# Output product on pairs of weight chunks, and other places for the second norm's steps, in a streaming encoder layer

## The reference

```python
def _mixers(h, st, p):
    ...
    merged = (g[:, :, 0] * (y_a @ p['w_br_ssd']) + g[:, :, 1] * (y_b @ p['w_br_gla'])
              + g[:, :, 2] * (y_c @ p['w_br_ml']))
    return merged @ p['w_out'], (...)

def _layer(x, c, st, p):
    ...
    x = x + g1 * _rmsnorm(mix, p['g_post_mix'])
    h = _rmsnorm(x, p['g_pre_ffn']) * (1.0 + sc2) + sh2
    f = (jax.nn.silu(h @ p['w_ffn_gate']) * (h @ p['w_ffn_up'])) @ p['w_ffn_down']
    x = x + g2 * _rmsnorm(f, p['g_post_ffn'])
```

## Time and profile before

| | |
|---|---|
| median of 3 runs | 1731.3 us (1730.98 to 1731.34) |
| the profiled execution's own time | 1731.23 us |
| its span, first to last instruction | 1729.0 us |
| PE busy | 1682.0 us, 97% |
| DVE busy | 1013.5 us, 59% |
| ACT busy | 641.3 us, 37% |
| output product, first matmul to the FFN's first | 1221.56 to 1285.36 us of the span |

### The profile page before, as it was taken

The page is one execution under the profiler, slowest core; times in us unless marked ns, Lnnn a source line. Parts: engine busy times, 40 slices in busy tenths (PEclk is TensorE's granted clock), DMA queues, the critical chain, the costliest instruction groups (busy, mean ns, idle before and its releaser), DMA issues.

```text
span 1729.0 us, 29185 instructions
## 1 busy us (share of the span) xinstructions
PE 1682.0 (97%) x11296; PEld 1543.6 (89%) x11296; DVE 1013.5 (59%) x1860; ACT 641.3 (37%) x1306; POOL 86.4 (5%) x160
## 2 busy tenths in 40 slices
PE   6999999999999999999999999999999999999997
PEld 4879898787899997899998899999999999999996
DVE  3745356644655554443533434555667788878886
ACT  5423333333433332333434343232343343343342
POOL 0000000000222220000000000000010000000001
PEclk8999999999999999999999999999999999999998
DMA  9862233575344346844546846445341223233224
GB/s 343 310 218 88 98 114 108 163 214 189 135 155 132 106 133 205 266 143 149 164 162 199 267 165 215 156 152 171 87 133 50 74 76 96 76 96 91 81 74 158
DMA packets 237752, 259.79 MB, mean 150 GB/s; under 512 B 14791, under 2 KB 212871, under 8 KB 235568
## 3 DMA queue, kind: packets, MB, share of 16 engines
q1 hardware_dynamic: 213550, 228.88, 41.6%
q10 hardware_dynamic: 24066, 29.06, 4.8%
HBM read 196.73 MB, written 61.17 MB: 149 GB/s over the span
## 4 chain that ended last, share of the span: by engine, by line
PE 57%; issue 29%; DVE 3%; PEld 3%; DMA 2%; ACT 1%; DVEq 1%; SPq 1%; POOLq 0%; POOL 0%; ACTq 0%; PEldq 0%
PE pj_acc L478 10%; PE pj_acc L480 10%; PE pj_acc L479 10%; PE pj_acc L490 5%; PE pj_acc L492 5%; PE pj_acc L491 5%; PE mx L1944 2%; PEld pj_acc L480 1%; PEld pj_acc L478 1%; PEld pj_acc L479 1%; PE mx L2432 1%; DMA hd_w<-in_w_ada 1%; PE mx L2423 1%; PE mx L2478 1%; PE mx L2703 1%
## 5 line engine op out<-in xcount | busy, mean ns | idle before, releaser
L478 PE MATMUL pj_acc<-pj_act_hi,pj_lo 128*128 128x320 f32 x1176 | 378.6, 322 | 2.1 <-DVE pj_lo L397 1.0
L480 PE MATMUL pj_acc<-pj_act_hi,pj_hi 128*128 128x320 f32 x1176 | 363.4, 309 | 0.0
L479 PE MATMUL pj_acc<-pj_act_lo,pj_hi 128*128 128x320 f32 x1176 | 363.1, 309 | 0.0
L478 PEld LDWEIGHTS pj_acc<-pj_act_hi,pj_lo 128*128 128x128 f32 x1176 | 220.9, 188 | 23.3 <-issue 19.9
L479 PEld LDWEIGHTS pj_acc<-pj_act_lo,pj_hi 128*128 128x128 f32 x1176 | 221.0, 188 | 3.8 <-issue 3.3
L480 PEld LDWEIGHTS pj_acc<-pj_act_hi,pj_hi 128*128 128x128 f32 x1176 | 220.7, 188 | 0.0
L397 DVE TENSOR_TENSOR pj_lo<-pj_raw,pj_hi 128x1024 fp32r<-128x1024 f32 (+1 forms) x136 | 165.7, 1222 | 83.2 <-ACT pj_hi L388 79.5
L490 PE MATMUL pj_acc<-pj_lo,pj_act_hi 128*128 128x256 f32 (+1 forms) x560 | 190.4, 340 | 3.2 <-DVE pj_lo L397 2.6
L492 PE MATMUL pj_acc<-pj_hi,pj_act_hi 128*128 128x256 f32 (+1 forms) x560 | 184.5, 329 | 0.0
L491 PE MATMUL pj_acc<-pj_hi,pj_act_lo 128*128 128x256 f32 (+1 forms) x560 | 184.2, 329 | 0.0
L388 ACT ACTIVATE pj_hi<-pj_raw 128x1024 fp32r<-128x1024 f32 (+1 forms) x136 | 141.8, 1052 | 37.3 <-PE pj_acc L480 34.2
(11 more groups left out here) (437 smaller groups left out, 3238.0 us busy)
## 6 DMA issues: line engine op xcount, KB each, us to landing
pj_raw<-in_w_in SPq DMA_DIRECT2D x50, 1024.0 KB, 5.7
ar_w<-in_w_ada SPq DMA_DIRECT2D x16, 1024.0 KB, 7.4
pj_raw<-in_w_ffn_gate SPq DMA_DIRECT2D x22, 512.0 KB, 4.0
pj_raw<-in_w_ffn_up SPq DMA_DIRECT2D x22, 512.0 KB, 5.4
pj_raw<-in_w_ffn_down SPq DMA_DIRECT2D x11, 1024.0 KB, 5.0
hd_w<-in_w_ada SPq DMA_DIRECT2D x16, 512.0 KB, 11.7
pm<-pj_tm_out ACTq DMA_DIRECT2D x30, 256.0 KB, 2.0
pt<-pj_cm_out ACTq DMA_DIRECT2D x48, 160.0 KB, 1.9
```

Of the source, the lines that this page charges most:

```text
L478: nc.tensor.matmul(out, lo[:, k, col], ahi[:, k, tok], start=(k == 0), stop=False)
L479: nc.tensor.matmul(out, hi[:, k, col], alo[:, k, tok], start=False, stop=False)
L480: last = nc.tensor.matmul(out, hi[:, k, col], ahi[:, k, tok], start=False, stop=(k == KT - 1))
```

## The change

The output product runs mostly in wide units. The chunks are listed in the order 1, 0, 2, 3 and paired (1 with 0, 2 with 3). The list of units becomes: chunk 1 with tiles 0 and 1, chunk 0 with tiles 0 and 1 (four narrow units), the pair 2, 3 with tiles 0 and 1 (wide), then for each of the tiles 2, 3 and 4 the pair 1, 0 and the pair 2, 3 (wide): 4 narrow and 8 wide units in place of 20 narrow ones. Splits of chunks 2 and 3 come one unit apart (they stood together), the second half of chunk 0's split a unit later than the first, and a unit now waits for the two halves of its weights one after the other. `take` copies 512 columns of a wide unit at once.

The steps of `Norm` get their places from a table. A place is counted in slots: a narrow unit is one slot, a wide unit two (its halves). The output stage has 20 slots before and after. `root`, `sum`, `scale` of tile t follow slots `at`, `at + 1`, `at + 2` with at = 5, 8, 11, 15, 19; `turn` follows slot `at + 4`, for the last tile `at + 3`. So turn 0 comes behind slot 9 (it was 6), turn 1 behind 12 (10), turn 2 behind 15 (14), turn 3 behind 19 (18), turn 4 behind 22 (22). Where two steps share a slot (turn 0 and sum 1, turn 1 and sum 2, turn 2 and root 3, turn 3 and root 4), the turn stands first in `plan`.

```diff
@@ def wide(self, u):
         n, x = self.units[u]
-        return self.chunks[n].mate is not None and x in self.BOTH
+        c = self.chunks[n]
+        return c.mate is not None and (x >= 2 or n != self.first_of("out") if c.how == "out" else x in self.BOTH)
@@ def span(self, u):
-        return (self.chunks[c.mate].dst, 2 * CW) if self.wide(u) else (c.dst, CW)
+        return (min(c.dst, self.chunks[c.mate].dst), 2 * CW) if self.wide(u) else (c.dst, CW)
@@ def tabulate(self):
-                self.splits[u_out + 1] += [(n, 0), (n, 1)]
+                self.splits[u_out + 1 + far] += [(n, 0), (n, 1)]
@@ def multiply(self, pe, u, part=None):
-        elif u == self.first[n] and c.how not in self.TM:
+        elif u == self.first[n] and c.kind == "CM":
@@
-            if self.wide(u):
+            if self.wide(u) and self.slot[n] < 2:
...
+            elif self.wide(u):
+                assert (self.slot[n], self.slot[c.mate]) == (2, 3)
+                hi, lo = (w[:, :, 0:2 * CW] for w in self.merge.yt[0])
@@ class Norm
-    STEPS = [(k, t) for t in range(NT) for k in ("root", "sum", "scale", "turn")]
+    AT = {(k, t): at + j + (j == 3 and t + 1 < NT) for t, at in enumerate((5, 8, 11, 15, 19))
+          for j, k in enumerate(("root", "sum", "scale", "turn"))}
+    STEPS = sorted(AT, key=AT.get)
@@ def take
-        self.nc.scalar.activation(self.mix[:, t % 2, c:c + CW], acc, ACT.Copy).then_inc(read, 1)
+        self.nc.scalar.activation(self.mix[:, t % 2, span[0]:span[0] + span[1]], acc[:, 0:span[1]], ACT.Copy
+                                  ).then_inc(read, 1)
@@ def layer
-    for u in range(u_out, len(proj.units)):
-        plan.append((None, u))
-        v = u - u_out - 3
-        plan += [(norm, s) for k, s in enumerate(norm.STEPS) if v == 4 * (k // 4) + k % 4]
+    for v, slot in enumerate(slots(u_out, len(proj.units))):
+        plan.append(slot)
+        part, u = slot
+        plan += [(norm, s) for s in norm.STEPS if v == norm.AT[s]]
@@ def projection_chunks
-    order += [(base - 4 + c, t) for t in range(NT) for c in range(4)]
+    order += [(base - 4 + c, t) for c in range(3) for t in range(2)]
+    order += [(base - 4 + c, t) for t in range(2, NT) for c in (0, 2)]
```

More of the change, by code:

```diff
@@ L480, in multiply @@
                 last = nc.tensor.matmul(out, hi[:, k, col], ahi[:, k, tok], start=False, stop=(k == KT - 1))
-        elif c.how in self.TM:
+        else:
             tok = slice(x * P, (x + 1) * P)
             out = self.out(u)[:, 0:self.span(u)[1]]
-            if self.wide(u):
+            if self.wide(u) and self.slot[n] < 2:
                 assert (self.slot[c.mate], self.slot[n]) == (0, 1)
@@ L494, in multiply @@
                 return
[L495 to L501, removed]
         last.then_inc(self.acc_full, 1)
@@ L558, in act_unit @@
             act.wait_ge(self.acc_full, u + 1)
-            self.norm.take(act, x, c.dst, acc[:, 0:CW], read)
+            self.norm.take(act, x, self.span(u), acc, read)
         elif c.how == "wino":
@@ L2840, in x1_stored, with take @@
                 eng.wait_ge(self.m.sem("x1_out%d" % s), 16 * ((tiles - s + 1) // 2))
-    def take(self, act, t, c, acc, read):
+    def take(self, act, t, span, acc, read):
         if t >= 2:
@@ L3354, in layer @@
     ssd.PREV, gla.PREV, mlstm.PREV, merge.PREV, norm.PREV = (conv, ada, small), (ssd,), (gla,), (mlstm,), (merge,)
+    for name in ("squared", "x1", "moved", "hi", "h"):
+        norm.m.sem(name)
     proj.mo_bias_in = sems.sem("mo_bias")
@@ L3527, in projection_chunks @@
         chunks += [Chunk("CM", "merge", [(0, CW, cols(a[name][0], n * CW))], n * CW) for n in range(4)]
-    chunks += [Chunk("TM", "out", [(0, CW, cols(a["w_out"][0], n * CW))], n * CW) for n in range(4)]
+    for n, c in enumerate((1, 0, 2, 3)):
+        chunks.append(Chunk("TM", "out", [(0, CW, cols(a["w_out"][0], c * CW))], c * CW,
+                            mate=len(chunks) + 1 if n % 2 == 0 else None))
     base = len(chunks)
```

## The result

The changed kernel takes **1734.94 us** (median of 17 runs, 1732.81 to 1736.01); the kernel before, measured beside it, 1731.3 us (17 runs, 1729.88 to 1732.47). The ratio is **1.0020, 95% interval 1.0013 to 1.0027**: slower by 0.2%, at the edge of what a measurement of this kernel can tell. The forecast was 1733.5 us in 1729.5 to 1736.0. The profiled execution took 1733.71 us, 2.48 more than the profiled one of before.

A forecast was written before the change was run, and what follows sets the result against it. PE, 97% busy, was taken as the bound, level with the ring. Savings of 2.4 and 2.2 us were outweighed by new waits: turn 4 +2.3 us on 1731.23 gave 1733.5 us, 0.13% slower, range 1729.5 to 1736.0.

The forecast's parts named there:

- turn 4's clock: PE's start of tile 4's transposes, in the FFN's entry: 1298.6 instead of 1296.33, 2.3 us later, carried to the end.
- early weight wait: PE's wait for chunk 1's weights early in the output stage, 0.74 us before, would go.
- turn 0 on PE: Tile 0's transposes in the output stage: PE reaches them at 1249.36, h ready 2.2 us early, no wait.
- DVE from turn to turn: One round of DVE's work between two tiles' turns in the output stage: 10.57 us without the root's wait.
- wait at turns 1 and 2: PE has 9.08 us of work between these transposes in the output stage, so waits 1.49 us for h at each.
- the FFN's first matmul: PE starts the FFN at 1284.85, held by weight splits on DVE, still 0.5 us ahead of before.
- the matmul at 1316.72: Later FFN matmul with a weight wait before: it and all the rest would move by 2.3 us.
- The ring: Output stage cycle making h: DVE turn, sum, squares and root, scale, PE transposes; 12.39 us before, 10.57 after, then the bound.
- The matmuls' term: Output stage: 192 wide matmuls at 0.2267 us replace narrow pairs at 0.2392, saving 2.4 us of PE.
- The ring does not bind: Faster rival: a round fits in 9.08 us, no waits at turns 1 to 3, stage ends 5.1 us earlier, 1726.1; chance 0.09.
- The delay is absorbed later: Rival: the FFN's 0.99 us weight-split wait does not follow PE's delay, 1 us comes back, 1732.5; chance 0.14.
- Transfers or stalls lengthen the ring: Slower rival: a late store of tile 0 or a DVE stall adds time in the output stage, 1735 to 1736; chance 0.20.

The follow-up runs named there:

- e2: Changed kernel, but in a slot shared by two steps the turn stands last, behind the next tile's sum or root: 1728.9 us, ratio 0.9985.
- e3: As e2, with tile 3's turn also moved one slot on, behind tile 4's sum: 1728.5 us, ratio 0.9982 to the kernel before.
- e6: The changed kernel run once more, unaltered: 1735.46 us, ratio 1.0017 to the kernel before.
- e7: Changed kernel, with SyncE storing a finished x1 tile before loading the next residual tile: 1735.13 us, ratio 1.0016 to the kernel before.
- e8: Kernel before, narrow units, turns of tiles 0 to 2 two slots later, ahead of the next tile's sum: 1744.42 us, ratio 1.0076.
- e9: As e8, narrow units, but these turns stand behind the next tile's sum: 1732.79 us, ratio 1.0007 to the kernel before.
- e4: Changed kernel, with only tile 3's turn moved behind tile 4's sum: 1734.07 us, ratio 1.0013 to the kernel before.
- e1: Changed kernel, with each turn directly behind its own scale, the extra slot undone: 1738.36 us, ratio 1.0038 to the kernel before.
- e5: Kernel before, narrow units, turns of tiles 0 to 3 one slot later, ahead of the next root: 1737.32 us, ratio 1.0031.

## Why the prediction was right

Its number rested on turn 4's clock, and that held. Step by step, profiled execution against profiled execution:

| step | predicted | measured |
|---|---|---|
| early weight wait | gone | gone |
| turn 0 on PE | 1249.36, no wait | 1249.53, no wait |
| DVE from turn to turn | 10.57 | 10.47, 10.82 |
| wait at turns 1 and 2 | 1.49, 1.49 | 1.03, 1.38 |
| turn 1, turn 2, turn 3 | 1259.93, 1270.50, 1282.5 | 1259.94, 1270.75, 1282.85 |
| the FFN's first matmul | 1284.85 | 1285.18 |
| turn 3 on DVE | 1285.97 | 1286.18 |
| turn 4 on PE | 1298.6 | 1298.87 |
| the matmul at 1316.72 | +2.3 | +2.54 |

Both columns count from the span's start. The measured output stage began 0.23 us earlier than that of before, so counted from the stage's start every measured time lies 0.23 us further behind its forecast than the table shows.

*The mechanism.* The change leaves three slots between turns 0, 1 and 2, where there were four. So PE's work between two turns fell from 12.4 to 9.4 us (10.41 less the wait of 1.03), most of it a slot's products and only the rest the matmuls' width. The ring lost only its wait for the root, 12.39 to 10.47 us, because on DVE the turn stayed ahead of the next sum. The difference became waits. e2 shows it by the other order: the waits go, and the time falls below that of before.

*The matmuls' term was mis-sized.* I took 0.2267 us for a wide matmul from another projection and 2.4 us for the lot. Timeline of PE in the changed kernel, the start of 24 wide matmuls that read their weights from the merge stage's buffer (mg_yt), then of some that read pj buffers:

```profile
1250.64 0.40 PE L495 MATMUL pj_acc<-mg_yt_hi,pj_act_lo 128*128 128x512 f32 x1
...
1256.03 0.39 PE L494 MATMUL pj_acc<-pj_lo,pj_act_hi 128*128 128x512 f32 x1
1256.26 0.39 PE L495 MATMUL pj_acc<-pj_hi,pj_act_lo 128*128 128x512 f32 x1
...
1258.52 0.39 PE L496 MATMUL pj_acc<-pj_hi,pj_act_hi 128*128 128x512 f32 x1
```

That is 5.39 / 23 = 0.2343 us from mg_yt, for five of the eight wide units, and 2.26 / 10 = 0.226 from pj, for three. The narrow matmuls of before differ too. I had measured them in a unit that reads pj, but half of the units read mg_yt; the first and the last matmul of two such units of the kernel before:

```profile
1239.97 0.28 PE L499 MATMUL pj_acc<-mg_yt_lo,pj_act_hi 128*128 128x256 f32 x1
...
1242.67 0.28 PE L501 MATMUL pj_acc<-mg_yt_hi,pj_act_hi 128*128 128x256 f32 x1
...
1252.23 0.28 PE L499 MATMUL pj_acc<-mg_yt_lo,pj_act_hi 128*128 128x256 f32 x1
...
1254.96 0.28 PE L501 MATMUL pj_acc<-mg_yt_hi,pj_act_hi 128*128 128x256 f32 x1
```

That is 0.1174 and 0.1187 us, two together 0.2348 to 0.2374. So a wide matmul saves 0.0005 to 0.003 us from mg_yt and 0.013 from pj, in all 120 x 0.0005 (or 0.003) + 72 x 0.013 = 1.0 to 1.3 us, not 2.4.

What of this reached the end is what stood ahead of turn 0, where the ring starts: PE came to turn 0 28.20 us after the stage's start, not 27.80. The rest only made PE come later to its turns and wait less there (1.03 us instead of 1.49 at turn 1). Turn 4 came 77.54 us after the stage's start, 0.50 later than the forecast's 77.04: 0.40 from turn 0, and the rest from the rounds, the first of which was shorter than forecast and the second longer, by the stall.

The Trainium skill, page "TensorE: Matmul & The Clock Gate", section "Back-to-back issue gap", has a formula for the gap of a matmul by itself, by which two matmuls of 256 columns take 2.5 ns more than one of 512 (an estimate). For mg_yt the measured 0.5 to 3 ns agree with that and not with my 12.5; for pj, 13 ns, they do not. By that formula a matmul of 512 columns takes 216 ns, less than was measured from either buffer.

*Sums on the way.* The pieces given for tile 0 add up to x1 at 1243.9 and h at 1246.9, not 1244.2 and 1247.2; nothing hangs on the 0.3 us.

*The rivals.* "The ring does not bind" fell with the waits at turns 1 and 2; e2 and e3 are that rival made real, and they gain 3 us where it promised 5.1, since the wide matmuls save less, and since then turn 4 waits 1.18 us for h (e2) or the FFN's first matmul 0.59 us for weights (e3). "The delay is absorbed later" fell: the wait of 0.99 us travels with the delay, in every wide and narrow kernel here. "Transfers or stalls lengthen the ring" was half there. ACT did wait for the store once, but e6 and e7 show no cost of the store. The stall was no accident of one execution: 0.44 to 0.46 us of it stand in DVE's turn of tile 1 in all twelve profiles, so it belonged in the sum; turn 2 waited 1.38 us instead of 1.03.

*What stays open.* By the shift the loss is 2.8 us, by three pairs of medians 2.9 to 3.6. The remainder is within the spread of either kernel's runs (about 3 us). The profiled executions differ by up to 5.2 us in when the output stage starts, ahead of everything that was reordered, so this spread may be all of it; no experiment shows that. With wide units the turns were never set four slots apart, so what the closer places cost by themselves is not shown. Nor did any run ask why a wide matmul is slower and a narrow one faster when it reads mg_yt, or what the stall is.

## What to carry to other kernels

When work is taken off a bound engine between two steps of a cycle that runs over other engines, because the work shrinks or because the steps move closer, first measure the cycle: from the moment it is the longer one, what is taken away comes back as a wait. Then look at the order on each engine of the cycle, not only on the one whose step was renumbered: here putting the turn behind the step that shares its slot, on VectorE and ScalarE, was worth 6 us, and the wider matmuls about 1. And a step that waits on ScalarE holds the accumulator copies queued behind it: nearly the same order that cost 2.8 us with wide units cost 14 with narrow ones (e8), partly through waits for these copies.

## What the runs showed of the hardware

- *The granted clock falls behind some single waits in a busy stream.* After PE waits of 2.20 us (e9), 2.24 (e4), 2.45 (e8) and 3.06 (e1) it was 0.83 over 10 us, 0.65 over 4.9, 0.83 over 10 and 0.86 over 12; after 2.13 us in e5 and after 2.63 us in e1 it stayed at 1.00. So the length of the wait alone did not decide. Behind the changed kernel's waits of 1.0 to 1.5 us it stayed at 1.00. In each of these four falls 1.7 us of PE's work was lost on top of the wait. At the lower level, 1.2 GHz, matmuls of 512 columns followed each other after 0.43 us.
- *The buffer that the weights come from shows in a matmul's pace*: at 512 columns 0.2343 us from mg_yt against 0.226 from pj; at 256 columns the other way, 0.1174 to 0.1187 against 0.1196.
- ScalarE's copy of 512 columns took 0.60 us, a narrow one 0.39.
